# Score products of a stick-breaking attention, cut into four 64x64 quarters with a copy of far keys and queries

## What is computed

```python
z = q_i @ k.T / sqrt(64)                       # one block of 128 queries against all keys
mask = k_pos[None, :] < t_pos[:, None]
log_fail = where(mask, log_sigmoid(-z), 0.0)
suffix = cumsum(log_fail, reverse=True) - log_fail
a = where(mask, exp(log_sigmoid(z) + suffix), 0.0)
out = a @ v
```

## Time and profile before

| | |
|---|---|
| median of three runs | 2819.62 us (2819.19 to 2821.75) |
| the profiled execution's own time | 2824.97 us |
| span in the profiled execution, first to last instruction | 2823.1 us |
| mean granted TensorE clock in it | 0.985 of full |
| PE busy | 2699.1 us, 96% of the span |
| DVE, POOL, ACT busy | 48%, 33%, 24% |

### The profile page before, as it was taken

The page is one execution under the profiler, slowest core; times in us unless marked ns, Lnnn a source line. Parts: engine busy times, 40 slices in busy tenths (PEclk is TensorE's granted clock), DMA queues, the critical chain, the costliest instruction groups (busy, mean ns, idle before and its releaser), DMA issues.

```text
span 2823.1 us, 50266 instructions
## 1 busy us (share of the span) xinstructions
PE 2699.1 (96%) x21508; PEld 2115.2 (75%) x21508; DVE 1341.4 (48%) x1291; ACT 684.6 (24%) x964; POOL 935.8 (33%) x414
## 2 busy tenths in 40 slices
PE   7999999999999999999999989998999999998987
PEld 6677778888888888888888756666677777776765
DVE  7844452214522122212366754343656565544588
ACT  3333340001211000000033334443131312112231
POOL 4322114444444344434444311113111221223466
PEclk9999999999999999999999999999999999999998
DMA  3100001112111111111122200001111110113443
GB/s 128 38 31 30 22 15 52 45 52 105 45 52 45 52 45 52 45 52 45 52 75 79 85 23 16 15 15 62 39 37 43 35 52 32 50 43 128 118 151 110
DMA packets 40749, 156.15 MB, mean 55 GB/s; under 512 B 4640, under 2 KB 5152, under 8 KB 39200
## 3 DMA queue, kind: packets, MB, share of 16 engines
q1 hardware_dynamic: 31392, 110.21, 12.1%
q10 hardware_dynamic: 9216, 43.78, 4.2%
HBM read 133.00 MB, written 20.97 MB: 55 GB/s over the span
## 4 chain that ended last, share of the span: by engine, by line
PE 85%; DVE 8%; issue 3%; ACT 3%; DMA 1%; POOL 1%; ACTq 0%; DVEq 0%; POOLq 0%; SPq 0%
PE dps L287 51%; PE dps L304 14%; PE aps L1684 6%; PE aps L1310 3%; PE aps L598 2%; PE dps L618 2%; PE dps L1323 1%; PE dps L609 1%; DVE h_lo L347 1%; PE dps L1331 1%; ACT mla_pt L1446 1%; DVE x_res L2528 1%; DVE sumsq L377 1%; PE aps L1587 1%; PE aps L1843 1%
## 5 line engine op out<-in xcount | busy, mean ns | idle before, releaser
L2601 POOL TENSOR_TENSOR w_hi<-w_raw,one 128x1024 fp32r<-128x1024 f32 x199 | 388.9, 1954 | 1843.1 <-PE dps L287 1323.3
L287 PE MATMUL dps<-h_hi,w_hi 128*128 128x512 f32 x1712 | 545.4, 395 | 25.2 <-POOL w_lo L2610 9.5
L287 PE MATMUL dps<-h_lo,w_hi 128*128 128x512 f32 x1712 | 539.5, 391 | 0.0
L287 PE MATMUL dps<-h_hi,w_lo 128*128 128x512 f32 x1712 | 539.2, 391 | 0.0
L2603 POOL TENSOR_TENSOR w_lo<-w_raw,w_hi 128x1024 fp32r<-128x1024 f32 x199 | 525.4, 2640 | 15.6
L287 PEld LDWEIGHTS dps<-h_hi,w_hi 128*128 128x128 f32 x1712 | 322.0, 189 | 100.6 <-issue 14.1
L287 PEld LDWEIGHTS dps<-h_hi,w_lo 128*128 128x128 f32 x1712 | 323.2, 189 | 68.1
L287 PEld LDWEIGHTS dps<-h_lo,w_hi 128*128 128x128 f32 x1712 | 323.3, 189 | 67.7 <-issue 0.2
L304 PE MATMUL dps<-h_hi,w_hi 128*128 128x512 f32 x528 | 181.5, 416 | 5.8 <-ACT rw_b L2140 2.5
L304 PE MATMUL dps<-h_lo,w_hi 128*128 128x512 f32 x528 | 178.1, 406 | 4.1 <-DVE rw_xm L2036 3.3
L304 PE MATMUL dps<-h_hi,w_lo 128*128 128x512 f32 x528 | 174.3, 408 | 1.2 <-DVE rw_akt L2052 1.1
(11 more groups left out here) (371 smaller groups left out, 4025.8 us busy)
## 6 DMA issues: line engine op xcount, KB each, us to landing
w_raw<-w_stream SPq DMA_DIRECT2D x200, 512.0 KB, 3.5
x_again<-x_t ACTq DMA_DIRECT2D x2, 4096.0 KB, 13.4
gates<-gate_out ACTq DMA_DIRECT2D x16, 512.0 KB, 2.7
tmp<-gates ACTq DMA_DIRECT2D x15, 512.0 KB, 4.1
x_t<-x_res ACTq DMA_DIRECT2D x4, 1024.0 KB, 3.9
out_t<-x_again SPq DMA_DIRECT2D x16, 256.0 KB, 2.0
back<-branches ACTq DMA_DIRECT2D x7, 512.0 KB, 8.2
x_res<-x_t ACTq DMA_DIRECT2D x2, 1536.0 KB, 12.0
```

The source lines that it names most:

```text
L287: mm = k.nc.tensor.matmul(k.dps[0:rows, pair, h * HALF:(h + 1) * HALF], w[:, slot, sub + t, 0:rows], x(t)[:, h * HALF:(h + 1) * HALF], sta ...
L2601: g.tensor_tensor(k.w_hi[:, s], k.w_raw[:, s], ones, ALU.mult).then_inc(k.sem("w_hi_done"), 1)
```

## The change

The queries are kept once, both heads on 128 partitions (`sb_q`), so the zero halves and their memsets go. Two copies with the heads exchanged between partition halves are added: `sb_qx` for queries 512 to 1023, and `sb_kx` for keys 320 to 1023 (`CROSSED` = 320). The scores of a unit become, after a mask product that now comes first, products of 64 contraction rows by 64 queries: for a long unit four of them, two per half of the queries, where the nearer-to-zero half of the keys (`near` = w/2) is taken from the head's own partitions and the other half from the exchanged copies; for a short unit two, both from the head's own partitions. `sb_z` places a long unit so that the middle of its keys lies on the border of the two PSUM banks. On DVE the second half of `sb_k` gives way to two exchanged copies of 704 columns, one ahead of unit 0 and one behind the multiplication of unit 0; the latter now increments `pair0_out`.

```diff
-    k.sb_q = [k.at(f"sb_q{h}", X + 4 * h * kb, [S]) for h in range(2)]
-    k.sb_k = k.at("sb_k", X + 8 * kb, [S])
+    k.sb_q = k.at("sb_q", X, [S])
+    k.sb_qx = k.at("sb_qx", X + 4 * kb, [HALF])
+    k.sb_k = k.at("sb_k", X + 6 * kb, [HALF])
+    k.sb_kx = k.at("sb_kx", X + 8 * kb, [S - CROSSED])
...
-    k.nc.vector.memset(k.zero[:, :], 0.0)
-    k.nc.vector.memset(k.sb_q[0][HD:P, :], 0.0)
-    k.nc.vector.memset(k.sb_q[1][0:HD, :], 0.0).then_inc(k.sem("sb_pad_done"), 1)
+    k.nc.vector.memset(k.zero[:, :], 0.0).then_inc(k.sem("zero_set"), 1)
...
+CROSSED = (SMALL + 1) * P // 2
...
 def sb_z(k, u):
-    return sb_part(k.aps[:, :, :].rearrange("p a b -> p (a b)"), u)
+    w = (UNITS[u][1] + 1) * P
+    lo = HALVES[u][0] * HALF + (HALF - w // 2 if w > HALF else 0)
+    return k.aps[:, :, :].rearrange("p a b -> p (a b)")[:, lo:lo + w]
...
-        for lo in range(0, (b + 1) * P, HALF):
-            hi = min(lo + HALF, (b + 1) * P)
-            mm = mul(sb_z(k, u)[:, lo:hi], k.sb_q[h][:, b * P:(b + 1) * P], k.sb_k[:, lo:hi],
-                     start=True, stop=False, skip_group_check=True)
-        mm = mul(sb_z(k, u)[:, b * P:(b + 1) * P], k.ident_r[:, :], k.sb_mask_r[:, :], start=False, stop=True, skip_group_check=True)
+        w = (b + 1) * P
+        near = w // 2 if b >= SMALL else w
+        own, across = HEADS[h], HEADS[1 - h]
+        z = sb_z(k, u)
+        mul(z[:, b * P:w], k.ident_r[:, :], k.sb_mask_r[:, :], start=True, stop=False, skip_group_check=True)
+        for m, queries in enumerate(HEADS):
+            at = b * P + m * HD
+            mm = mul(z[queries, 0:near], k.sb_q[own, at:at + HD], k.sb_k[own, 0:near],
+                     start=near < w, stop=True, skip_group_check=True)
+            if near < w:
+                mm = mul(z[queries, near:w], k.sb_qx[across, at - HALF:at - HALF + HD], k.sb_kx[across, near - CROSSED:w - CROSSED],
+                         start=False, stop=True, skip_group_check=True)
         mm.then_inc(k.sem("sb_z_done"), 1)
...
-    for h, head in enumerate(HEADS):
-        ins = v.scalar_tensor_tensor(k.sb_q[h][head, :], k.dps[head, 1, :], HD ** -0.5, k.inv[head, :], ALU.mult, ALU.mult)
+    v.scalar_tensor_tensor(k.sb_q[:, :], k.dps[:, 1, :], HD ** -0.5, k.inv[:, :], ALU.mult, ALU.mult)
+    for own, across in (HEADS, HEADS[::-1]):
+        ins = v.scalar_tensor_tensor(k.sb_qx[across, :], k.dps[own, 1, HALF:], HD ** -0.5, k.inv[own, HALF:], ALU.mult, ALU.mult)
     ins.then_inc(k.sem("pair1_out"), 1)
     dve.wait_ge(k.sem("blk_done"), blk + n_k)
-    for t, done in ((slice(0, HALF), "sb_k_done"), (slice(HALF, S), "pair0_out")):
-        v.tensor_tensor(k.sb_k[:, t], k.dps[:, 0, t], k.inv[:, t], ALU.mult).then_inc(k.sem(done), 1)
+    v.tensor_tensor(k.sb_k[:, :], k.dps[:, 0, 0:HALF], k.inv[:, 0:HALF], ALU.mult).then_inc(k.sem("sb_k_done"), 1)
+
+    def keys_across(own, across):
+        return v.tensor_tensor(k.sb_kx[across, :], k.dps[own, 0, CROSSED:], k.inv[own, CROSSED:], ALU.mult)
+
+    keys_across(*HEADS)
     if before is None:
         branch()
     for u in range(N_UNITS):
...
         v.tensor_tensor(a[:, 0:w - 1], a[:, 0:w - 1], fail[:, 1:w], ALU.mult).then_inc(k.sem("sb_a_done"), 1)
+        if u == 0:
+            keys_across(*HEADS[::-1]).then_inc(k.sem("pair0_out"), 1)
```

More of the change, by code:

```diff
@@ L545, in sb_pe @@
 def sb_pe(k, pe):
-    pe.wait_ge(k.sem("sb_pad_done"), 1)
     pe.wait_ge(k.sem("masks_done"), 3)
@@ L639, in sb_dve @@
 def sb_dve(k, dve):
-    dve.wait_ge(k.sem("sb_pad_done"), 1)
+    dve.wait_ge(k.sem("zero_set"), 1)
     dve.sem_inc(k.sem("sb_y_done"), 1)
```

## The result

| | before | after |
|---|---|---|
| median of the runs made side by side | 2820.33 us (2815.3 to 2823.15, 19 runs) | 2825.02 us (2823.4 to 2826.99, 19 runs) |
| ratio, 95% interval | | 1.0019 (1.0012 to 1.0025) |
| profiled execution, own time / span | 2824.97 / 2823.1 us | 2826.34 / 2824.5 us |
| mean granted clock in it | 0.985 | 0.982 |

The change costs 0.19%, some 4.7 us, where a gain of 5.3 us was forecast. 2825 lies outside the range of 2809.5 to 2820.5. By the bound of 0.2% that I had set, the interval lies across the border between "the same" and "slower", and it excludes a gain.

What follows compares the result with a forecast made beforehand. PE, busy 96% of the span, was taken as the bound, with DVE close behind. Pairs 1 to 3 give -3.3 us and pair 0 -2.0, together -5.3: median 2819.62 to 2814.3 us, range 2809.5 to 2820.5.

Steps and rivals of the forecast that it cites:

- Overlap of quarters: Long units' scores on PE: four quarters run side by side, halving the streaming, 0.85 us less for w = 1024.
- The rival in which only neighbours overlap: Half products start in strict program order, so score quarters partly queue: 2849 us; slower by missing overlap had 5%.
- the one in which column halves are read in turn: Quarters share the array but two column halves' moving data is read one after the other; no chance of its own.
- Changes of shape: PE switching from mask to quarters and back to full-array turns: 0.31 us per unit, both borders together.
- The step, and DVE as the next limit: Two full units in the middle fall from 4.26 to about 3.6 us, level with DVE's 3.6, without DVE idling.
- The crossed copy: DVE at a pair's start: 704 columns take 0.89 us, the second copy uncovered, first turn about 0.9 later.
- the rival in which DVE's copy costs nothing: PE was the only bound, so each pair gains 0.9 us more: 2810.7 us, chance 11%.
- The sum for pairs 1 to 3: Unit-by-unit change in when scores are ready, ending at -1.1 us per pair, -3.3 for three.
- four times 0.31 given back: Units 12 to 15, short and on a full PE, each lose 0.31 us to the changes between array shapes.
- the 0.1 at the last turns: End of a pair: 0.1 us less given back, because PE waits a little at the last turns.
- The clock in pairs 1 to 3: Stages of pairs 1 to 3 taken at full clock; a fall with PE idling longer was listed only as disproof.
- Pair 0: First pair's stage, partly at half clock, where saved streaming counts twice: -2.0 us, between -0.8 and -3.8.

Runs made afterwards that it cites:

- before_late_keys: Kernel before, with the second half of the keys written behind unit 0's multiplication, nothing in quarters; 2824.55 us, 1.0013 of the kernel before.
- after_filled: Changed kernel plus full-array products nobody reads where PE idles at the start of a pair; 2815.81 us, 0.9990 of the kernel before.
- before_filled: Kernel before plus unread full-array products where PE waits at the start of a pair; 2822.27 us, 1.0009 of the kernel before.
- before_short_quarters: Kernel before, with only short units' scores as a mask and two quarter products; 2831.80 us, 1.0047 of the kernel before.
- after_filled_quarters: Changed kernel with PE's idle places filled mostly by unread products of two diagonal quarters; 2822.97 us, 1.0005 of the kernel before.
- both_filled: Changed kernel with both crossed key copies ahead of unit 0, short units full-array, and unread full-array filling; 2815.84 us, 0.9983 of the kernel before.

## Why the prediction was wrong

**Overlap of quarters: right.** It was the largest term and the one with a rule against it. All four quarters run side by side (starts 123.94 to 123.96, then 124.42 to 124.44). The rival in which only neighbours overlap is excluded, and so is the one in which column halves are read in turn. By the Trainium skill, "TensorE: Matmul & The Clock Gate", Part 3, matmuls keep strict program order. For whole products the trace does not contradict it (they start at 123.94, .95, .95 and .96); for the two halves of a 32-bit product, as the rival had read it, it does: the second halves start only at 124.42, behind the first halves of all four.

**Changes of shape: right in size.** Going in, the second halves start 0.48 us behind the first where they stream 0.43, the 0.05 of the forecast; coming out, the last halves start at 124.44, end their 0.43 at 124.87, and the turn starts 0.09 later, as taken. The group as a whole is 0.61 us shorter (1.88 against 1.27); the forecast was 0.85 - 0.31 = 0.54.

**The step, and DVE as the next limit: right.** 3.59 us against 3.6, DVE without idling.

**The crossed copy: right.** 0.888 us against 0.89, and it stands open: the first turn comes 1.0 later against 0.9. before_late_keys prices 0.68 us of lateness at 0.6 per stage, so the rival in which DVE's copy costs nothing falls.

**The sum for pairs 1 to 3: right where its condition holds.** after_filled has the condition, full clock, and shows -1.0, -1.1, -1.1. The working does not add up to its own result, though: from -2.55 at unit 11, four times 0.31 given back leave -1.3, and the 0.1 at the last turns makes that -1.2 or -1.4, not -1.1. That -1.1 was met so closely is therefore partly luck; the steps are good to 0.1 to 0.3 us a pair. (The forecast named stages of 43.7 against 44.8; that is the same difference, measured from another point.)

**The clock in pairs 1 to 3: the step that failed.** The sum took it as full. The prediction had only "if the clock falls in stages of pairs 1 to 3, where PE now idles longer" among what would make it wrong; it got no price and no chance. Measured, 6.8 to 10.2 us at half clock in each stage turned -1.1 into +0.9, +0.8 and +0.8 (47.52, 47.36 and 46.22 against 46.60, 46.57 and 45.43) and, in the second execution, +1.8, 0.0 and +1.6. Against after_filled the fall costs 1.9 us in each of the three (47.52 - 45.59, 47.36 - 45.43, 46.22 - 44.32). A bound on the price could have been had from the rows of before: pair 0 has half clock in the stage, and takes some 5 us more than pair 1. Not all of that is the clock: in before_filled pair 0 has full clock and still takes 3.2 us more than pair 1 (49.85 against 46.62).

The reason that I gave with it was wrong as well. Idling alone does not do it (before_late_keys: later first turn, full clock). Quarters in the short units alone do, with no more idling (before_short_quarters). Of the 12 stages of pairs 1 to 3 profiled with full-array scores none has half clock; of the 18 with quarters and no filling all have; of the six with quarters and full-array filling none has; with quarter filling two of three have. The time that PE is busy, which I read, does not tell the clock: 2.68 of 3.40 us in quarters was followed by half clock, 2.27 of 3.40 in the shape of before was not; 3.40 of 3.40 mostly in quarters was (after_filled_quarters), 1.65 of 3.40 on the full array was not (before_late_keys). The Trainium skill, "TensorE: Matmul & The Clock Gate", Part 1, has the gate follow how busy PE has been recently; these rows agree only if products on one or two quarters of the array count for less than products on all of it.

Which part of the change carries it is not one part. Each was undone alone and the fall stayed: without the late copy, and without the short units in quarters. In the change as made it is the short units: in both executions and all three pairs the clock falls ahead of the first turn or with it, before any long unit of the pair has run, so nothing that saves streaming has part in it. With the short units back on the full array the fall comes later, behind the first long unit's quarters. With both edits it still stays. The 0.46 us by which unit 0's scan under POOL still delays the first turn are not the cause by themselves, since before_late_keys has 0.68 us of delay at full clock; so it takes the long units' quarters as well. Whether they would be enough without any delay is not shown. Nor is it shown how: four of them run side by side on the whole array, and the ends of PE's records are modelled, so that 1.87 us busy against 1.65 leaves room for a small difference in work.

**Pair 0.** The forecast was -2.0. The two profiles of before differ there by 2.5 us (53.33 and 50.88, with 10.2 and 3.4 us of half clock), those of after are 50.38 and 49.33. On the means that is -2.2, but a difference of two executions each, no more than in line with the forecast.

**What stays open.** The stages do not account for the whole loss. Their sum is 191.9 and 189.5 us in the two profiles of before, 191.5 and 191.3 in those of after: +0.7 on the means, against +4.7 of the median. In these four profiles most of the rest lies behind them (+3.1 on the means). From the first turning of pair 3's results to the end pass 2425.7 and 2423.5 us in the two executions of before, 2428.8 and 2426.7 in those of after. The program there is the same; the profiles differ in stretches at half clock, such as 1624.4 to 1634.6, which after has at 0.51 and the second execution of before at 1.00. But before_filled has such a stretch as well and 2428.9 us, and after_filled and both_filled have 2423.9. Runs of one kernel differ in it too, as the two groups of after_filled show (0.988 against 0.984, 7 us apart). Whether the change makes such stretches behind the stages more frequent, and how, was not tried. Of the 10 us between the forecast change (-5.3) and the measured (+4.7), the clock in the stages of pairs 1 to 3 is shown to hold 5.7 (three times 1.9). Some 3 more lie behind the stages in the profiles, which differ there in the clock; the last 1 or so is not placed. With the filling the median falls by some 8 us (ratios 1.0019 and 0.9990), more than those 5.7, so part of the rest goes with it.

## What to carry to other kernels

A product cut into pieces that share the array saves streaming as the overlap says, but pieces that leave part of the array idle count for less toward TensorE's clock in these runs; before betting on it, look at the granted clock where PE already idles and price its fall, by a stage that has one. If the clock falls, put full-array products that nobody reads into the waits: here that turned +0.19% into -0.10%. A part that gains nothing from the new shape (the short units) should keep the old one, and a copy that the first consumer waits for should not stand behind an operation that another engine can hold up.

## What had not been expected of the hardware

- PE can be busy without a gap and the clock still fall: 3.40 of 3.40 us, mostly in quarter products, ahead of half clock from 350.1 on (after_filled_quarters). And it can be busy for 1.65 of 3.40 us with full-array products at full clock (before_late_keys). That PE is busy throughout while at half clock says nothing of the shape: the kernel before has it with full-array products, 5.00 of 5.00 us at 0.50.
- A scan of 128 columns with both inputs in SBUF that starts while POOL makes `w_lo` also takes 2.17 us instead of its share of 0.29 (2.29 us for 1024 columns), just as the multiplication did. Moving a copy ahead of the multiplication therefore only moved the stand-still to the scan.
- A copy crossed between the partition halves costs no more than the forecast took from the straight one: 0.888 us for 704 columns, where 0.686 for 512 gives 0.94 at most.
